# Three squared-ReLU MLPs of 256 tokens: one 512-column matmul on high and low activations side by side in the place of two 256-column ones, drains that add two halves

## What is computed

```python
def sqrelu_mlp(x, w1, w2):
    h = jax.nn.relu(x @ w1)
    return (h * h) @ w2

for layer in range(DEPTH):                       # first block, DEPTH = 2
    ...                                          # a mixer, a layer norm
    x = layer_norm(DN_ALPHA * x + sqrelu_mlp(x, mlp_w1[layer], mlp_w2[layer]), ln2_g[layer], ln2_b[layer])
...
    h2 = modulate(rmsnorm(xl_new, g_pre_mlp[i]), ml[3], ml[4])          # second block
    xl_new = xl_new + ml[5] * rmsnorm(sqrelu_mlp_2(h2, w_mlp_in[i], w_mlp_out[i]), g_post_mlp[i])
```

## Time and profile before

| | |
|---|---|
| runs, us | 1698.59, 1698.73, 1696.48 (median 1698.59) |
| the profiled execution | 1697.05 us, of which the span is 1695.1 us |
| TensorE matmul busy | 1612.7 us, 95% of the span |
| TensorE weight load busy (overlaps the matmuls) | 1412.3 us, 83% |
| VectorE, ScalarE, GpSimd busy | 998.8, 838.5, 76.3 us (59%, 49%, 4%) |
| mean granted TensorE clock | 0.984 of full speed |

### The profile page before, as it was taken

One profiled execution on the slowest core, in us unless ns is written; L12 is line 12 of the kernel. 1 busy time (PEld: TensorE's weight loads), 2 busy tenths in 40 slices (PEclk: granted clock), 3 DMA queues, 4 the chain that ended last, 5 costly groups with the idle time before them and its releaser, 6 DMA issues.

```text
span 1695.1 us, 26811 instructions
## 1 busy us (share of the span) xinstructions
PE 1612.7 (95%) x10898; PEld 1412.3 (83%) x10898; DVE 998.8 (59%) x1532; ACT 838.5 (49%) x1484; POOL 76.3 (4%) x60
## 2 busy tenths in 40 slices
PE   7998999999999999999989999999999988889997
PEld 7887789998889999987557588888888874789997
DVE  6854865556686566679764653333333687565555
ACT  5434175553826566353574551524243455665554
POOL 1200300001030000000000100000000100000000
PEclk9999999999999999999999999999999998999999
DMA  8723765556756555533101532232222241235551
GB/s 311 271 108 125 261 230 181 186 181 216 273 174 223 175 187 186 195 141 100 50 1 62 211 100 100 87 99 99 99 87 87 75 137 38 66 122 175 186 185 49
DMA packets 69939, 247.53 MB, mean 146 GB/s; under 512 B 7504, under 2 KB 10576, under 8 KB 69712
## 3 DMA queue, kind: packets, MB, share of 16 engines
q1 hardware_dynamic: 69840, 246.18, 42.4%
HBM read 245.10 MB, written 1.05 MB: 145 GB/s over the span
## 4 chain that ended last, share of the span: by engine, by line
PE 76%; DVE 12%; issue 7%; ACT 4%; DMA 0%; POOL 0%; DVEq 0%; SPq 0%; ACTq 0%; POOLq 0%
PE psum L375 20%; PE psum L377 19%; PE psum L376 19%; DVE lo_ring L336 2%; PE psum L1122 2%; PE psum L1774 2%; PE psum L390 1%; PE psum L391 1%; PE psum L392 1%; DVE c_conf L2052 1%; PE psum L1797 1%; PE psum L1784 1%; PE psum L490 1%; PE psum L403 1%; DVE h_conv L892 1%
## 5 line engine op out<-in xcount | busy, mean ns | idle before, releaser
L375 PE MATMUL psum<-x_hi,hi_ring 128*128 128x256 f32 (+1 forms) x1464 | 460.5, 315 | 11.7 <-DVE x_lo L881 9.6
L336 DVE TENSOR_TENSOR lo_ring<-raw_ring,hi_ring 128x1024 fp32r<-128x1024 f32 x348 | 433.0, 1245 | 60.2 <-PE psum L377 21.1
L377 PE MATMUL psum<-x_hi,lo_ring 128*128 128x256 f32 (+1 forms) x1464 | 455.9, 311 | 0.0
L376 PE MATMUL psum<-x_lo,hi_ring 128*128 128x256 f32 (+1 forms) x1464 | 455.8, 311 | 0.0
L348 ACT ACTIVATE hi_ring<-raw_ring 128x1024 fp32r<-128x1024 f32 x292 | 307.5, 1054 | 262.9 <-PE psum L377 248.3
L375 PEld LDWEIGHTS psum<-x_hi,hi_ring 128*128 128x128 f32 x1464 | 280.9, 192 | 33.6 <-issue 16.0
L375 PE MATMUL psum<-hid_hi,hi_ring 128*128 128x256 f32 (+1 forms) x992 | 303.4, 306 | 0.3 <-DVE lo_ring L336 0.3
L377 PE MATMUL psum<-hid_hi,lo_ring 128*128 128x256 f32 (+1 forms) x992 | 302.1, 305 | 0.0
L376 PE MATMUL psum<-hid_lo,hi_ring 128*128 128x256 f32 (+1 forms) x992 | 301.2, 304 | 0.0
L376 PEld LDWEIGHTS psum<-x_lo,hi_ring 128*128 128x128 f32 x1464 | 281.0, 192 | 14.9 <-issue 0.2
L377 PEld LDWEIGHTS psum<-x_hi,lo_ring 128*128 128x128 f32 x1464 | 280.9, 192 | 14.7
(11 more groups left out here) (424 smaller groups left out, 2008.2 us busy)
## 6 DMA issues: line engine op xcount, KB each, us to landing
raw_ring<-weights SPq DMA_DIRECT2D x460, 512.0 KB, 3.4
h_const<-hyb_consts SPq DMA_DIRECT2D x1, 1088.0 KB, 11.6
x<-xT SPq DMA_DIRECT2D x1, 1024.0 KB, 6.6
x<-ctxT SPq DMA_DIRECT2D x1, 1024.0 KB, 16.8
outT<-x SPq DMA_DIRECT2D x4, 256.0 KB, 2.5
shared<-shared_consts SPq DMA_DIRECT2D x1, 398.0 KB, 13.4
par<-params SPq DMA_DIRECT2D x1, 301.5 KB, 6.7
```

What stands on the lines that cost most here:

```text
L336: nc.vector.tensor_tensor(lo_ring[:, s, :], raw_ring[:, UNIT_AT[u] % RAW_SLOTS, :], hi_ring[:, s, :].bitcast(F32), ALU.subtract).then_inc( ...
L375: nc.tensor.matmul(bank(u % BANKS, T), w_hi, hi[:, k, 0:T], start=(k == 0), stop=False)
L376: nc.tensor.matmul(bank(u % BANKS, T), w_hi, lo[:, k, 0:T], start=False, stop=False)
L377: last = nc.tensor.matmul(bank(u % BANKS, T), w_lo, hi[:, k, 0:T], start=False, stop=(k == KT - 1))
```

## The change

For a T = 256 MLP and j < 7, a unit is run by the new `unit_in_halves`: the high and low activations lie in one tile (`x_parts`, `hid_parts`, `[P, 2, KT, TB]`), and one matmul of 512 columns with the high weights writes high-high into the first half of the bank and high-low into the second half. One matmul of 256 columns with the low weights adds low-high to the first half. The two halves then have to be added. For W2 units VectorE adds each half to `y` in turn, with the low weight part between the two. For W1 units VectorE reduces the two halves into `hid_sum`, and ScalarE takes the ReLU from there. j = 7 stays as it was, as do the three interleaved units and the MLP on 512 tokens. That makes 25 W1 and 28 W2 units in each of MLPs 0, 1 and 3, 159 units in all.

```diff
-    x_hi = nc.alloc_sbuf_tensor("x_hi", [P, KT, TB], F32R)
-    x_lo = nc.alloc_sbuf_tensor("x_lo", [P, KT, TB], F32R)
+    x_parts = nc.alloc_sbuf_tensor("x_parts", [P, 2, KT, TB], F32R)
+    x_hi, x_lo = x_parts[:, 0], x_parts[:, 1]
...
+    def side_by_side(u):
+
+        return bank(u % BANKS).rearrange("p (s t) -> p s t", s=2)
+
+    def unit_in_halves(pe, u, parts, first=None, n=None, turn=None):
...
+        for k in range(KT):
+            if first:
+                first(k)
+            w_hi, w_lo = hi_ring[:, s, k * P:(k + 1) * P], lo_ring[:, s, k * P:(k + 1) * P]
+            nc.tensor.matmul(side_by_side(u), w_hi, parts[:, :, k, 0:SEQ], start=(k == 0), stop=False)
+            last = nc.tensor.matmul(bank(u % BANKS, SEQ), w_lo, parts[:, 0, k, 0:SEQ], start=False, stop=(k == KT - 1))
...
+    hid_sum = relu[:, :, SEQ:TB]
...
+    def hidden_in_halves(T, i, j):
+
+        return in_halves(T, j) and (i > 0 or j >= WIDE_FIRST)
...
-                nc.scalar.activation(relu[:, j % 2, 0:T], bank(u % BANKS, T), ACT.Relu).then_inc(drained[u % BANKS], 1)
-                wait_drained(act, u)
+                if hidden_in_halves(T, i, j):
+                    wait_drained(act, u)
+                    link(nc.scalar.activation(relu[:, j % 2, 0:T], hid_sum[:, j % 2, :], ACT.Relu))
...
+        def next_hidden_lo(i, j):
+            u = base + 2 * KT * i + j
+            if i:
+                next_lo(dve, u)
+            elif j < KT - 1:
+                next_lo(dve, u + 1)
...
+                if hidden_in_halves(T, i, j):
+                    u = first + j
+                    wait_unit(dve, u)
+                    nc.vector.tensor_reduce(hid_sum[:, j % 2, :], side_by_side(u).rearrange("p s t -> p t s"), AX.X,
+                                            ALU.add).then_inc(drained[u % BANKS], 1)
+                    next_hidden_lo(i, j)
+                    hidden_low(i, j)
+                else:
+                    hidden_low(i, j)
+                    next_hidden_lo(i, j)
...
+                if in_halves(T, j):
+                    nc.vector.tensor_tensor(y[:, j, 0:T], side_by_side(u)[:, 0], y[:, j, 0:T], ALU.add).then_inc(flag("half_added"), 1)
+                    next_lo(dve, u)
+                    now["half_added"] += 1
+                    dve.wait_ge(flag("half_added"), now["half_added"])
+                    nc.vector.tensor_tensor(y[:, j, 0:T], side_by_side(u)[:, 1], y[:, j, 0:T], ALU.add).then_inc(drained[u % BANKS], 1)
```

More of the change, by code:

```diff
@@ L196, in program @@
     r = Region(M0, END)
[L197 to L198 removed]
+    hid_parts = r("hid_parts", [P, 2, KT, TB], F32R)
+    hid_hi, hid_lo = hid_parts[:, 0], hid_parts[:, 1]
     relu = r("relu", [P, 2, TB])
@@ L377, in unit @@
             last = nc.tensor.matmul(bank(u % BANKS, T), w_lo, hi[:, k, 0:T], start=False, stop=(k == KT - 1))
+        last.then_inc(unit_done, 1)
+    def side_by_side(u):
+        return bank(u % BANKS).rearrange("p (s t) -> p s t", s=2)
+    def unit_in_halves(pe, u, parts, first=None, n=None, turn=None):
+        n = u if n is None else n
+        turn = u // BANKS if turn is None else turn
+        pe.wait_ge(lo_ready, n + (SPLIT[u] - u) + 1)
+        if u >= BANKS:
+            pe.wait_ge(drained[u % BANKS], turn)
+        s = SPLIT[u] % SPLIT_SLOTS
+        for k in range(KT):
[4 more added lines that the diff above has]
+            last = nc.tensor.matmul(bank(u % BANKS, SEQ), w_lo, parts[:, 0, k, 0:SEQ], start=False, stop=(k == KT - 1))
         last.then_inc(unit_done, 1)
@@ L1267, in gated_dve, with in_halves @@
             nc.vector.tensor_tensor(x[:, a:b, 0:T], t, x[:, a:b, 0:T], ALU.add).then_inc(flag("x_updated"), b - a)
+    def in_halves(T, j):
+        return T == SEQ and j < KT - 1
     def mlp_pe(pe, m, base, T, s, late=False):
@@ L1272, in quarter @@
             turn = lambda u: i * 4 + u // BANKS
-            for u in range(base + done, base + KT):
-                unit(pe, u, x_hi, x_lo, T, n=i * 16 + u, turn=turn(u))
+            for j in range(done, KT):
+                u = base + j
+                if in_halves(T, j):
+                    unit_in_halves(pe, u, x_parts, n=i * 16 + u, turn=turn(u))
+                else:
+                    unit(pe, u, x_hi, x_lo, T, n=i * 16 + u, turn=turn(u))
             for j in range(full):
                 u = base + KT + j
-                unit(pe, u, hid_hi, hid_lo, T,
-                     first=(lambda k: pe.wait_ge(flag("hidden_ready"), i * KT + (KT * QUARTERS * m + k + 1))) if j == 0 else None,
-                     n=i * 16 + u, turn=turn(u))
+                block_of = (lambda k: pe.wait_ge(flag("hidden_ready"), i * KT + (KT * QUARTERS * m + k + 1))) if j == 0 else None
+                if in_halves(T, j):
+                    unit_in_halves(pe, u, hid_parts, first=block_of, n=i * 16 + u, turn=turn(u))
+                else:
+                    unit(pe, u, hid_hi, hid_lo, T, first=block_of, n=i * 16 + u, turn=turn(u))
         first_units(pe, base, x_hi, x_lo, T, lambda k: pe.wait_ge(x_ready, KT * (s + 1) + k + 1), width=WIDE_FIRST)
@@ L1368, in late_scaled_dve @@
         lo(KT - 1)
+    hid_sum = relu[:, :, SEQ:TB]
+    now["half_added"] = 0
+    def hidden_in_halves(T, i, j):
+        return in_halves(T, j) and (i > 0 or j >= WIDE_FIRST)
     def mlp_act(act, link, m, base, T):
@@ L1389, in mlp_dve, with hidden_low @@
     def mlp_dve(dve, link, m, base, T):
+        def hidden_low(i, j):
+            dve.wait_ge(flag("hidden_hi"), KT * (QUARTERS * m + i) + j + 1)
+            nc.vector.tensor_tensor(hid_lo[:, j, 0:T], relu2[:, j % 2, 0:T], hid_hi[:, j, 0:T].bitcast(F32),
+                                    ALU.subtract).then_inc(flag("hidden_ready"), 1)
+        def next_hidden_lo(i, j):
[4 more added lines that the diff above has]
+                next_lo(dve, u + 1)
         for i in range(QUARTERS):
@@ L1407, in mlp_dve @@
                 wait_unit(dve, u)
-                nc.vector.tensor_tensor(y[:, j, 0:W], bank(u % BANKS, W), y[:, j, 0:W], ALU.add).then_inc(drained[u % BANKS], 1)
-                next_lo(dve, u)
+                if in_halves(T, j):
+                    nc.vector.tensor_tensor(y[:, j, 0:T], side_by_side(u)[:, 0], y[:, j, 0:T], ALU.add).then_inc(flag("half_added"), 1)
[3 more added lines that the diff above has]
+                    nc.vector.tensor_tensor(y[:, j, 0:T], side_by_side(u)[:, 1], y[:, j, 0:T], ALU.add).then_inc(drained[u % BANKS], 1)
+                else:
+                    nc.vector.tensor_tensor(y[:, j, 0:W], bank(u % BANKS, W), y[:, j, 0:W], ALU.add).then_inc(drained[u % BANKS], 1)
+                    next_lo(dve, u)
                 if i == QUARTERS - 1 and m < 2:
```

5 lines of the change are left out of this document (4 added, 1 removed).

## The result

The changed kernel took 1721.78 us (median of four runs, 1719.17 to 1725.52), the kernel before 1697.58 (the three runs of the table and one more of 1696.57): a ratio of 1.0139, 95% interval 1.0126 to 1.0152. It is slower by 1.4%. The profiled execution's span is 1720.0 us against 1695.1, 24.9 us more.

The account below looks back on a forecast made before the run. TensorE's matmuls were taken as the bound. Per MLP, 7.55 us delay less 3.6 saved gave 11.8 us for three; with 4.5 for the clock, 16.3 on 1697.05 made 1713.4, taken as 1714, range 1703 to 1725.

Parts of the forecast that it names:

- part 3: Quarter 0: VectorE and ScalarE form one chain, 4.34 us a block against TensorE's 2.8; second W2 unit 7.55 us late.
- The clock: Behind quarter 0's waits TensorE's clock falls to 1.2 GHz once per MLP, 1.5 us each, 4.5 us in all.
- The savings: One 512-column matmul replaces a 256-column pair: 0.105 us per W1 unit, 0.053 per W2 unit, 12.4 us if TensorE stays the bound.
- Part 2: Quarters 1 to 3: VectorE's added work, 2.2 of 2.78 us per W1 unit, is hidden by TensorE's next unit and costs nothing.
- the 1.3 us named in the prediction: Quarters 1 to 3: a reduction of 1.3 us or more would end the cover, each such unit costing the excess.
- Case (a): Rival, faster: TensorE never waits in quarter 0 and the 12.4 us come out, 1686 us; chance 0.08.
- Case (c): Rival, no change: removed changeovers carry more than the rows say and cancel the waits; chance 0.06.
- case (b): Rival, no gain from 512 columns: two pieces cost what two matmuls cost, 1726 us; little or no saving, chance 0.12.
- the case of 1722: Matmul spacing by the skill's formula: a step saves 2.5 ns, 1.0 us instead of 3.6 per MLP, some 1722 us.
- Case (d): Rival, the clock holds at full speed behind quarter 0's waits: 1710 us; chance 0.16.

Follow-up runs that it names:

- The first run: Changed kernel with quarter 0's W1 units back to the old way, all other units still in halves: 1688.53 us, ratio 0.9957 to the kernel before.
- its complement: Changed kernel with only quarter 0's 12 W1 units (j = 3 to 6) in halves, everything else the old way: 1726.33 us, ratio 1.0181.
- the reordered kernel: Changed kernel, all 159 units in halves, VectorE in quarter 0 writing unit u+3's low weight part instead of u+4's from block 3 on: 1688.52 us, ratio 0.9941.
- filling the waits: Changed kernel with 20 and 26 unread matmuls ahead of TensorE's waits for hidden blocks 5 and 6 in quarter 0: 1716.57 us, ratio 1.0125.
- Tripling it: Kernel with quarter 0's W1 units the old way, plus two more reductions ahead of each in quarters 1 to 3: 1768.67 us, ratio 1.0405.
- the two kernels that have only savings in them: Changed kernel with only the 84 W2 units in halves, 1694.47 us; with only the 63 W1 units of quarters 1 to 3 in halves, 1691.55 us.
- the run with the eighth unit: Kernel with VectorE's order in quarter 0 mended, now with j = 7 in halves too, 24 more units: 1698.68 us, ratio 1.0009.

## Why the prediction was right, point by point

**Direction and mechanism.** Slower was forecast, by the chain of part 3, and every link of it stands in the trace: the low weight part waiting for ScalarE, the ReLU for the reduction, reductions of j = 3 to 6 4.4 us apart, two long waits of TensorE in the first W2 unit. The first run and its complement show that the whole loss is there; the reordered kernel shows that the order of VectorE's work is the cause and not the work. The number is less good than the mechanism: its larger errors all go one way, and 1721.8 lies 3 us from the upper end of the range.

**The chain's size.** Expected 4.34 us a block, measured 4.41; 0.05 of the 0.07 lie at the handover from the reduction to the ReLU (0.77 us from start to start, 238.50 to 239.27, instead of 0.72). The second W2 unit was expected 7.55 us late. In MLP 0 it starts at 257.71 where it was 247.81, 9.9 us later, of which 1.3 are a later start of the stage (231.80 against 230.49): 8.6 us. The other 1.05 us are the chain (0.3) and for the most part the last two steps, which run at half clock already.

**The clock.** The direction was right, the term was the worst of the sum: 1.5 us per MLP were taken from one fall in the earlier trace rows, and filling the waits gave back 2.7, 1.6 and 2.6. The row that I took had 3.4 us at the lower level behind a wait of 2.1 us; here TensorE waited twice, and the lower level lasted until 4 to 6 us after the second wait. That row was not a sure one either: the same wait is in every run, and in four of them no fall follows it (last section). Of the 8 us by which 1714 falls short of 1721.8 this is about 2.4. The Trainium skill (TensorE: Matmul & The Clock Gate, "HAM oscillation") warns that waits which come between short bursts of matmuls let the clock fall. The trace agrees in part. The two waits have one step between them, and 1.2 GHz follows in all three MLPs; but in MLPs 0 and 3 the clock fell as the first wait ended (at 252.1 and 1545.8), before a second one and behind a long run of matmuls, and in MLP 1 within the second (at 566.2).

**The savings.** W1 was right (0.105 forecast, 0.107 measured per unit), W2 too high: 0.053 forecast, 0.036 measured. Its step of two matmuls takes 349 ns, not 346.8. Why is not shown; W1 reads two pieces too, and its step takes 346.6. That is 84 x 0.017 = 1.4 us over the kernel. So the sum's terms explain about 5 of the 8 us (2.4 for the clock, 0.9 for the chain, 1.4 here); of the rest, 1.3 us are the later start of MLP 0's stage in the one profiled run, and 1.7 us lie between the MLPs and behind them, where the change touches nothing but the tiles' place. They are not told apart from the spread of single executions: 1719 to 1726 us for the changed kernel, and in the profiled executions of all eleven kernels MLP 0's first plain W1 unit starts anywhere from 230.2 to 234.0.

**Part 2, costed at nothing,** held: no wait in quarters 1 to 3, the reduction at 0.68 to 0.69 us as the rows said. Tripling it shows that the cover was real and that it is used up somewhere between 0.7 and 2.1 us; the 1.3 us named in the prediction was not tried.

**The rivals.** Case (a), faster, was wrong for this kernel and right in direction for the same kernel with VectorE's order in quarter 0 changed: 12.4 us forecast, 9 to 10 measured. Case (c), no change, is excluded by the result. By its number alone, 1721.8 is nearer to two others than to the forecast: case (b), no saving, at 1726, and the case of 1722 that the prediction made from the Trainium skill's formula (TensorE: Matmul & The Clock Gate, "Back-to-back issue gap"). Both are excluded by the step's price: W1 saves 13.4 ns a step and W2 4.4 ns, where case (b) has 0 and the formula 2.5 for both, and the two kernels that have only savings in them are faster. That section gives the formula for a matmul by itself, and 131 ns at 512 columns for a stream with weight loads; the 226.9 to 229.0 ns of the earlier trace rows agree with neither. Case (d), the held clock, is excluded by the clock in the trace.

## What to carry to other kernels

When a step is put in front of an engine's old first step, follow what the instructions behind it wait for: here a new reduction made the ReLU wait for VectorE, and an old prefetch on VectorE already waited for ScalarE, so two engines that worked side by side took turns. Look at the prologue of a loop apart, since its prefetch distance may differ from the loop's; the time of a whole change can hang on one quarter of one stage. And a second drain may stand behind a prefetch as long as nobody waits for it, but not behind the last unit.

## What the runs showed of the hardware

**The price of the same pair of matmuls is not one number.** A step of a 512-column and a 256-column matmul took 347 ns in W1 and 349 in W2 in the changed kernel. With the waits filled it was 353 ns in the W1 stretches of MLPs 0 and 3 and 354 in their W2 stretches, at full clock, and 347 and 349 again in MLP 1. TensorE with the waits filled, two stretches of MLP 0 and one of MLP 1:

```profile
279.03 0.39 PE L396 MATMUL psum<-x_parts,hi_ring 128*128 128x512 f32 x1
...
301.69 0.40 PE L396 MATMUL psum<-hid_parts,hi_ring 128*128 128x512 f32 x1
...
324.31 0.39 PE L396 MATMUL psum<-x_parts,hi_ring 128*128 128x512 f32 x1
...
589.06 0.40 PE L396 MATMUL psum<-x_parts,hi_ring 128*128 128x512 f32 x1
...
611.35 0.40 PE L396 MATMUL psum<-hid_parts,hi_ring 128*128 128x512 f32 x1
```

22.66 and 22.62 us for W1 and W2 in MLP 0 (and in MLP 3), 22.29 for W1 in MLP 1. The W2 stretches of the run with the eighth unit have 353 ns as well. 353 ns is what three matmuls of 256 columns take in W2, and in W1 they take 360; so in such a stretch the change saves nothing in W2 and half in W1. What sets it stays open; no run here varies it alone. That the same tiles, read in the same way, go at 347 and at 353 ns also speaks against the prediction's case (b), where the 2 ns between two stretches were put down to the place of the operand.

**The lower clock outlasted the waits by 4 to 6 us.** In the changed kernel it was back 6.1, 4.1 and 5.8 us after the last wait in MLPs 0, 1 and 3; in the earlier trace rows it lasted 3.4 us. The two waits of a quarter thus cost up to 2.7 us beyond their length, measured by taking only the clock's fall away.

**The same wait brought a fall in some executions and not in others.** The wait of the earlier trace rows is there in all eleven kernels, 1.87 to 2.28 us long, in a stretch where the change touches nothing but the tiles' place. In seven profiled executions the clock fell as the wait ended or up to 1.4 us behind it, and in four it didn't. Here is one that didn't, the kernel with only the W1 units of quarters 1 to 3 in halves (timeline, then the stretch with its granted clock):

```profile
486.29 0.35 PE L410 MATMUL psum<-x_parts,hi_ring 128*128 128x256 f32 x1 [1.87 <-DVE x_parts L1207]
```

```profile
486.00:500.00 14.00, 13.71 (x114) 1.00 0.61 220
```

The length of the wait doesn't tell the two apart: 1.88 us brought a fall in one kernel, 1.95 us brought none in two. The longer waits of quarter 0 brought it each time, nine places in the three kernels that have them unfilled. So one such row is a price that may or may not be paid, and a forecast should give it a chance and not only a size.
